# Two layers of a decoder on one core: low parts, constant products and statistics at the layer norms moved

## Chip, core and metric

The kernel runs on one core of one Trainium2 chip. The metric is the device time of one execution in microseconds (us), the median over the runs.

## What is computed

A trunk of two layers makes one inference step for 512 prompt tokens and 8 sample tokens, held as one matrix of 520 columns and 1024 rows. Layer 0 mixes with a gated convolution and a matrix memory, layer 1 with two kinds of sparse attention; after each mixer and each MLP there is a layer norm over a scaled residual:

```python
yp = layer_norm(ALPHA * yp + mp, ln_g[layer, 0], ln_b[layer, 0])
yp = layer_norm(ALPHA * yp + sq_relu_mlp(yp, w_up[layer], w_down[layer]), ln_g[layer, 1], ln_b[layer, 1])

def layer_norm(x, g, b):
    mu = jnp.mean(xf, axis=-1, keepdims=True)
    var = jnp.mean(jnp.square(xf - mu), axis=-1, keepdims=True)
    y = (xf - mu) * lax.rsqrt(var + LN_EPS) * g + b

def sq_relu_mlp(x, w_up, w_down):
    return jnp.square(jax.nn.relu(x @ w_up)) @ w_down
```

The same holds for the sample tokens (`ys`). The MLP is 1024 x 4096 and back.

## The kernel before

Activations lie transposed: `xT` has the 1024 features in 8 blocks `k` of 128 partitions and the 520 tokens in two halves of 260 columns. Half 0 and half 1 go through the chip one behind the other wherever a norm stands between two matrix products.

Every large product is computed in three parts, since each operand is split into a rounded high part and the rest: high weight times high x, high weight times low x, low weight times high x. For an output tile of 128 rows and one half this makes 24 matmuls (8 blocks `k` times 3), each of 260 columns. High parts are written by ScalarE (ACT): `wr` for weights, `xh` for activations. Low parts are a subtraction: `ring_lo` for weights, by VectorE (DVE, `w_lo`, L2081), and `xl` for activations, by DVE (L2179) for the blocks 0, 2, 4, 6, 7 and by GpSimd (POOL, `x_low`, L854) for the blocks 1, 3, 5. Weights come from HBM in chunks of four tiles (2 MB) into three slots, loaded by SyncE's queue (SP) when the tile that used the slot last is done.

There are three such norms with a split result: norm 0 (behind the output projection of layer 0, ahead of its MLP), norm 1 (behind that MLP, ahead of layer 1's input projection) and norm 2 (behind the output projection of layer 1, ahead of its MLP). Ahead of a norm stands a "tail" on TensorE (PE): 8 tiles for half 0, then the same 8 tiles for half 1. Behind it stands a "head": 8 tiles of the MLP for half 0, then the same for half 1, of which the first four run together, block `k` by block `k`.

While the tail's tiles come out, each engine does its part of the norm, in an order that is written out by hand, one queue for each engine, with semaphores between them:

- DVE adds each tile to the residual (`residual`, L2092 and L2093). Between the tiles of half 1 it also works on half 0: `normed` (times 1/deviation, L2160), `x_lows` (L2177, L2179), and the low weights of the head's first four tiles (L2081).
- ACT squares the residual (L1705). Between the tiles of half 1 it scales half 0 (`scaled`, L1750), which gives `xh` and the blocks 1, 3, 5, 7 of `xT`, and copies the head's first weights (L1679).
- POOL adds up sums and squares over the tiles (`sums`, L820 to L825, two additions a tile), subtracts the mean from half 0 (`centre`, L832) and makes its three low parts (`x_low`, L854), one each behind the sums of tiles 4, 5 and 6 of half 1.
- PE multiplies the sums with a constant matrix `meanM` (`norm_sums`, the statistics): those of half 0 behind the first tail tile of half 1, those of half 1 behind head tile 0. They wait for POOL's last addition of the half.

At the start of the head PE also issues products of two constant matrices whose result nobody reads (`keep_busy`, L1027): 5 ahead of head tile 0 and 10 ahead of its block 2 at norms 0 and 2, 14 and 10 at norm 1. In the trace each of them is two instructions.

In the MLP's first part the other engines run `hidden(j)` for the head's tiles of half 0: ACT's relu, the copy of the weights of head tile j + 4 and the square `hh`; POOL's product `hid` (L866); DVE's low weights of tile j + 4 and the subtraction `hl` (L2110). Between them stand the steps of half 1 of the norm: ACT `moments`, `deviation`, `scaled`; DVE `variance`, `inverse`, `normed`, `x_lows`; POOL `centre`, `x_low`. Before the change `moments` and `variance` are the first thing in the queue, ahead of `hidden(0)`.

Head tile `i` from 4 on waits until ACT has read the bank of tile `i - 4`; in half 1 the same holds for DVE.

Of the kernel before, what the change touches and what calls it, by code (L numbers as in the profile page):

```python
# [29 lines left out]
KD = D // P  # L30
# [39 lines left out]
XL_POOL = (1, 3, 5)  # L70
# [7 lines left out]
def build(nc, x_prompt, x_sample, state_conv, state_C, state_n, state_m, cache_kv, cache_idx, cache_win, page_table,  # L78
# [20 lines left out]
    with ExitStack() as ctx:  # L99
# [522 lines left out]
        for branches, pairs in ((("d",), ((3, 0), (2, 1))), (("s", "w"), ((2, 0), (1, 3)))):  # L622
            for pair in pairs:
                for br in branches:
                    heads = [[(p, g) for p in range(NP) for g in range(2)] for _ in pair]
                    for n in last_turns if (pair, br) == ((1, 3), "w") else turns:
                        i = pair[n]
# [129 lines left out]
        def _(pool):  # L757
# [71 lines left out]
            def centre(n_ln, half, ms):  # L829
                pool.wait_ge(sm["mu_ok"], 2 * n_ln + half + 1)  # L830
                for m in ms:
                    pool.tensor_tensor(xT[:, m, cols(half)], xT[:, m, cols(half)], mu[:, cols(half)],  # L832
                                       ALU.subtract).then_inc(sm["cen_p"], 1)

            def norm(n_ln, g0):

                for i, (m, half) in enumerate(norm_order(n_ln)):
                    if m:
                        sums(n_ln, g0, m, half)
                    if (m, half) == (KD - 1, 0):  # L840
                        centre(n_ln, 0, range(KD))
                    if 2 * KD - 4 <= i < 2 * KD - 1:
                        x_low(n_ln, 0, (XL_POOL[i - 2 * KD + 4],))

            def split_y(k, s, v, y=ymix, at=0):

# [3 lines left out]
            def x_low(n_ln, half, ms):  # L850
                c = cols(half)
                for m in ms:
                    pool.wait_ge(sm["x_ready"], xr(n_ln, half) + XT_ACT.index(m) + 1)
                    pool.tensor_tensor(XL[n_ln][:, m, c], xT[:, m, c], XH[n_ln][:, m, c].bitcast(F32), ALU.subtract).then_inc(sm["xl_p"], 1)  # L854
# [13 lines left out]
            def mlp(layer, g):  # L868

                n_ln = 2 * layer  # L870
                for j in range(KD):
                    hidden(layer, g + j, 0, j, 0)
                    if j < 2:
                        centre(n_ln, 1, range(4 * j, 4 * j + 4))
                    if 3 <= j < 6:
                        x_low(n_ln, 1, (XL_POOL[j - 3],))
                for j in range(KD):
                    hidden(layer, g + j, 0, j, 1)
                for c in range(1, NFC):
                    for j in range(KD):  # L880
                        hidden(layer, g + 2 * KD * c + j, c, j)
# [7 lines left out]
            for idx in range(len(E_TILE)):  # L889
                g = G_IN0 + idx  # L890
                if 17 <= idx < 21:
                    i = idx - 17
# [125 lines left out]
        def _(pe):  # L1018
# [8 lines left out]
            def keep_busy(bank, n):  # L1027

                for _ in range(n):
                    mm(ps[bank][:, 0:P], ident[:, :], ones[:, :])  # L1030
# [57 lines left out]
            def head(n_ln, g):  # L1088

                n = HEADS[g]  # L1090
                keep_busy(3, 14 if n_ln == 1 else 5)
                hi_here = x_hi_here(n_ln, 0)

                def first_tile(k):
                    if k == 2:
                        keep_busy(3, 10)
                    hi_here(k)

                for i in range(n):
                    if i >= 4:  # L1100
                        pe.wait_ge(sm["free_a"], g + i - 3)
                    split_pass((g + i,), (0,), XH[n_ln], XL[n_ln], first_tile if i == 0 else None,
                               x_lo_here(n_ln, 0) if i == 0 else None)
                    if i == 0:
                        norm_sums(n_ln, 1)
                first = n // 2
                split_pass(range(g, g + first), (1,), XH[n_ln], XL[n_ln], x_hi_here(n_ln, 1), x_lo_here(n_ln, 1))
                for i in range(first, n):
                    if i >= 4:
                        pe.wait_ge(sm["free_b"], g + i - 3)  # L1110
                    split_pass((g + i,), (1,), XH[n_ln], XL[n_ln])
# [278 lines left out]
            for idx, name in enumerate(O_NAMES):  # L1390
# [6 lines left out]
                if 4 <= idx <= 6:  # L1397

                    n = idx - 4
                    i = 3 - n  # L1400
# [273 lines left out]
        def _(act):  # L1674
# [51 lines left out]

            def mlp(layer, g):
                n_ln = 2 * layer
                moments(n_ln, 1)
                for j in range(KD):  # L1730
                    hidden(layer, g + j, 0, j, 0)
                    if j == 0:
                        deviation(n_ln, 1)
                    if 1 <= j <= 4:
                        scaled(n_ln, 1, (2 * j - 2, 2 * j - 1))
                for j in range(KD):
                    hidden(layer, g + j, 0, j, 1)
                for c in range(NFC):
                    for j in range(KD if c else 0):
                        hidden(layer, g + j, c, j)  # L1740
                    g += KD
                    for j in range(KD if c < NFC - 1 else 0):
                        w_hi_ahead(g + j)
                    g += KD
                if layer == 0:
                    norm(1, g - KD)
# [6 lines left out]
            def moments(n_ln, half):  # L1753

                act.wait_ge(sm["stats_mm"], 2 * n_ln + half + 1)
                copy(mu[:, cols(half)], ps[4 * half][:, 0:H2]).then_inc(sm["mu_ok"], 1)
                act.activation(var[:, cols(half)], ps[4 * half][:, 0:H2], ACT.Square).then_inc(sm["sq_mu"], 1)

            def deviation(n_ln, half):
                act.wait_ge(sm["std_in"], 2 * n_ln + half + 1)  # L1760
                act.activation(rs[:, cols(half)], var[:, cols(half)], ACT.Sqrt).then_inc(sm["stats_ok"], 1)

            def scaled(n_ln, half, ms):

                for m in ms:
                    act.wait_ge(sm["cen_v"], KD * (2 * n_ln + half) + m + 1)
                    affine(XH[n_ln], n_ln, m, half).then_inc(sm["x_hi"], 1)
                    act.wait_ge(sm["x_hi"], KD * (2 * n_ln + half) + m + 1)
                    if m in XT_ACT:
                        affine(xT, n_ln, m, half).then_inc(sm["x_ready"], 1)  # L1770
# [172 lines left out]
            for idx, name in enumerate(O_NAMES):  # L1943
# [8 lines left out]
                if 4 <= idx <= 6:  # L1952
                    n = idx - 4
                    i = 3 - n
# [56 lines left out]
            for t in range(len(units) + 5):  # L2011
                if t < len(units):
                    i, p, g, br, k0, o = units[t]
# [9 lines left out]
                if 0 <= u < len(units):  # L2023
                    i, p, g, br, k0, o = units[u]
# [44 lines left out]
        def _(dve):  # L2069
# [43 lines left out]

            def mlp(layer, g):
                n_ln = 2 * layer
                variance(n_ln, 1)
                for j in range(KD):
                    hidden(layer, g + j, 0, j, 0)
                    if j == 0:
                        inverse(n_ln, 1)  # L2120
                    if j <= 4:
                        normed(n_ln, 1, NORMED[n_ln][j])
                        x_lows(n_ln, 1, LOWS[n_ln][j])
                for j in range(KD):
                    hidden(layer, g + j, 0, j, 1)
                for c in range(NFC):
                    for j in range(KD if c else 0):
                        hidden(layer, g + j, c, j)
                    g += KD
                    scale = ALPHA if c == 0 else None  # L2130
                    if c < NFC - 1:
                        for m in range(KD):
                            for half in range(2):
                                residual(g, m, half, scale)
                            w_lo_ahead(g + m)
                        g += KD
                    elif layer == 0:
                        norm(1, g, scale)
                    else:
                        last_norm(g)  # L2140

            def variance(n_ln, half):

                c = cols(half)
                dve.wait_ge(sm["sq_mu"], 2 * n_ln + half + 1)
                link(dve.tensor_tensor(var[:, c], ps[4 * half + 1][:, 0:H2], var[:, c], ALU.subtract))
                dve.tensor_scalar(var[:, c], var[:, c], 0.0, LN_EPS, ALU.max, ALU.add).then_inc(sm["std_in"], 1)

            def inverse(n_ln, half):
                dve.wait_ge(sm["stats_ok"], 2 * n_ln + half + 1)  # L2150
                dve.reciprocal(rs[:, cols(half)], rs[:, cols(half)]).then_inc(sm["std_ok"], 1)  # L2151

            def normed(n_ln, half, ms):

                c = cols(half)
                dve.wait_ge(sm["std_ok"], 2 * n_ln + half + 1)
                for m in ms:
                    x = xT[:, m, c]
                    dve.wait_ge(sm["cen_p"], KD * (2 * n_ln + half) + m + 1)
                    dve.tensor_tensor(x, x, rs[:, c], ALU.mult).then_inc(sm["cen_v"], 1)  # L2160

            def x_lows(n_ln, half, ms):
                for m in ms:
                    if m in XL_DVE:
                        x_low(n_ln, half, m)
# [239 lines left out]
            for idx, t in enumerate(E_TILE):  # L2405
# [40 lines left out]
                if idx >= 25:  # L2446
                    i = idx - 25
# [440 lines left out]
```

## Time and profile before

| | us |
|---|---|
| median of 3 runs | 1395.46 (1393.62 to 1395.48) |
| the profiled execution | 1396.67 |
| its span, first to last instruction | 1395.1 |

| engine | busy us | share of the span |
|---|---|---|
| PE, matmul | 1349.7 | 97% |
| PE, weight load | 1286.0 | 92% |
| DVE | 722.7 | 52% |
| ACT | 506.0 | 36% |
| POOL | 395.2 | 28% |

The profile comes from one execution. Busy time is the union of an engine's instructions; the end of a matmul is modelled, and matmuls overlap in the pipeline, so starts are the better measure on PE. "Granted clock" is the share of TensorE's full clock (2.4 GHz) that it was given; its mean is 0.988. In a timeline a bracket gives the idle time of the engine ahead of the instruction and the instruction that released it. Lines are those of the kernel before.

### The profile page before, as it was taken

How to read it: one execution, taken by the hardware profiler on the slowest of the kernel's cores; microseconds unless marked ns; L12 is line 12 of the kernel's file. 1: busy time of each engine (PE TensorE's matmuls, PEld its weight loads, DVE VectorE, ACT ScalarE, POOL GpSimd, SP SyncE). 2: the span in 40 equal slices, each digit the busy share in tenths (PEclk: the TensorE clock that was granted, in tenths of full speed). 3: DMA queues.
4: the chain of work that ended last, by engine and by line, in shares of the span. 5: the costliest groups of instructions: out<-in, count | busy, mean ns of one | idle time of the engine just before them, and what ended most of it. 6: DMA issues, size and time to landing. Idle time of an engine off the chain costs nothing. (4 is left out here: it accounts for less than half of the span.)

```text
span 1395.1 us, 27563 instructions
## 1 busy us (share of the span) xinstructions
PE 1349.7 (97%) x11310; PEld 1286.0 (92%) x11310; DVE 722.7 (52%) x1390; ACT 506.0 (36%) x1014; POOL 395.2 (28%) x467
## 2 busy tenths in 40 slices
PE   5999999999999999999999999999999999999996
PEld 5999999999999999999899766668999999999996
DVE  3425966774343343446789655553674343333435
ACT  3322236454031231234442467775453131230311
POOL 3013535652010010137534371025651010110102
PEclk9999999999999999999999899999999999999998
DMA  5351251213313131304331154212303222222201
GB/s 159 100 143 61 91 188 65 71 52 121 122 61 121 62 121 61 122 8 99 99 62 37 33 170 129 62 44 79 122 19 123 102 87 96 93 89 99 84 31 62
DMA packets 87101, 123.87 MB, mean 89 GB/s; under 512 B 24338, under 2 KB 42206, under 8 KB 86944
## 3 DMA queue, kind: packets, MB, share of 16 engines
q1 hardware_dynamic: 82048, 107.00, 24.0%
q0 software_dynamic: 4928, 15.10, 3.6%
q8 instruction: 91, 1.49, 0.4%
q14 instruction: 34, 0.28, 0.1%
HBM read 115.62 MB, written 8.57 MB: 89 GB/s over the span
## 5 line engine op out<-in xcount | busy, mean ns | idle before, releaser
L1063 PE MATMUL ps<-xh,ring_lo 128*128 128x260 f32 (+2 forms) x2496 | 504.6, 284 | 0.0
L1063 PEld LDWEIGHTS ps<-xh,ring_lo 128*128 128x128 f32 (+2 forms) x2496 | 383.6, 187 | 1.5 <-ACT big L1679 0.4
L1063 PE MATMUL ps<-xl,wr 128*128 128x260 f32 x1568 | 351.8, 283 | 6.1 <-DVE xl L2179 3.8
L1063 PE MATMUL ps<-xh,wr 128*128 128x260 f32 x1568 | 353.4, 284 | 1.4 <-DVE ring_lo L2081 1.0
L1063 PEld LDWEIGHTS ps<-xl,wr 128*128 128x128 f32 x1568 | 255.6, 188 | 7.8 <-DVE xl L2179 5.0
L1063 PEld LDWEIGHTS ps<-xh,wr 128*128 128x128 f32 x1568 | 256.3, 188 | 3.5 <-ACT att L1716 1.4
L866 POOL TENSOR_TENSOR att<-att 128x520 f32<-128x520 f32 (+1 forms) x80 | 77.3, 967 | 548.5 <-DVE att L2105 521.5
L2081 DVE TENSOR_TENSOR ring_lo<-ring,wr 128x1024 fp32r<-128x1024 f32 (+1 forms) x144 | 192.0, 1336 | 60.2 <-ACT wr L1679 60.1
L1063 PE MATMUL ps<-hh,wr 128*128 128x260 f32 x1024 | 222.1, 283 | 0.0
L1063 PE MATMUL ps<-hh,ring_lo 128*128 128x260 f32 x1024 | 221.8, 283 | 0.0
L1063 PE MATMUL ps<-hl,wr 128*128 128x260 f32 x1024 | 221.7, 283 | 0.0
L1679 ACT ACTIVATE wr<-ring 128x1024 fp32r<-128x1024 f32 (+1 forms) x162 | 167.9, 1050 | 130.0 <-PE ps L1063 119.7
L1063 PEld LDWEIGHTS ps<-hh,wr 128*128 128x128 f32 x1024 | 164.5, 188 | 0.2 <-issue 0.2
L1063 PEld LDWEIGHTS ps<-hh,ring_lo 128*128 128x128 f32 x1024 | 164.5, 188 | 0.0
L1063 PEld LDWEIGHTS ps<-hl,wr 128*128 128x128 f32 x1024 | 164.0, 188 | 0.0
L1716 ACT ACTIVATE att<-ps 128x260 f32<-128x260 f32 x64 | 24.6, 384 | 304.5 <-PE ps L1063 304.5
L2092 DVE TENSOR_TENSOR xT<-xT,ps 128x260 f32<-128x260 f32 x96 | 37.5, 421 | 162.9 <-PE ps L1063 162.9
L2105 DVE TENSOR_SCALAR att<-ps 128x260 f32<-128x260 f32 x64 | 27.3, 427 | 137.5 <-PE ps L1063 137.5
L1063 PE MATMUL ps<-hl,ring_lo 128*128 128x260 f32 (+1 forms) x464 | 93.5, 283 | 0.0
L1679 ACT ACTIVATE big<-ps 128x260 f32<-128x260 f32 (+6 forms) x104 | 40.3, 401 | 138.9 <-PE ps L1063 121.6
L813 POOL TENSOR_TENSOR ring_lo<-ring,wr 128x1024 fp32r<-128x1024 f32 x18 | 43.3, 2412 | 108.5 <-ACT wr L1679 108.5
L1025 PE MATMUL ps<-big 128*64 128x128 f32 (+3 forms) x504 | 67.0, 353 | 4.7 <-DVE small L2843 3.3
(356 smaller groups left out, 1581.1 us busy)
## 6 DMA issues: line engine op xcount, KB each, us to landing
ring<-in_w_up SPq DMA_DIRECT2D x16, 2048.0 KB, 7.9
ring<-in_w_down SPq DMA_DIRECT2D x16, 2048.0 KB, 7.9
ring<-in_w_in_e SPq DMA_DIRECT2D x9, 1024.0 KB, 6.8
ring<-in_w_in_e SPq DMA_DIRECT2D x2, 2048.0 KB, 8.7
ring<-in_w_out_e SPq DMA_DIRECT2D x2, 2048.0 KB, 9.4
ring<-in_w_in_o SPq DMA_DIRECT2D x16, 256.0 KB, 4.9
ring<-in_cache_kv POOLq DMA_DIRECT2D x32, 128.0 KB, 2.4
ring<-in_w_out_o SPq DMA_DIRECT2D x8, 512.0 KB, 7.9
```

The lines of the kernel that those rows point to most:

```text
L813: pool.tensor_tensor(w_l, w_raw(u), w_h.bitcast(F32), ALU.subtract).then_inc(sm["w_lo_p"], 1)
L866: pool.tensor_tensor(hid[j % 2][:, cc], rel[j % 2][:, cc], rel[j % 2][:, cc], ALU.mult).then_inc(sm["hid_sq"], 1)
L1025: return pe.matmul(out, lhsT, rhs, start=start, stop=stop, skip_group_check=True)
L1063: last = pe.matmul(bank(g, half)[0:width(g), 0:H2], w[:, k, :], x[:, k, cols(half)], start=first, stop=final)
L1679: return act.activation(out, in_, ACT.Copy, scale=scale)
L1716: act.activation(rel[j % 2][:, 0:H2], psA(g)[:, 0:H2], ACT.Relu).then_inc(sm["free_a"], 1)
L2081: dve.tensor_tensor(w_l, w_raw(u), w_h.bitcast(F32), ALU.subtract).then_inc(sm["w_lo"], 1)
L2092: last = (dve.tensor_tensor(x, x, y, ALU.add) if scale is None else dve.scalar_tensor_tensor(x, x, scale, y, ALU.mult, ALU.add))
L2105: dve.tensor_scalar(rel[j % 2][:, H2:T], psB(g)[:, 0:H2], 0.0, None, ALU.max).then_inc(sm["free_b"], 1)
```

## The change

Three things change at norms 0 and 2; norm 1 stays as it is. POOL's three low parts of half 0 stand behind the sums of tiles 3, 4 and 5 of half 1. PE issues no constant products there. The statistics of half 1 stand behind head tile 1, and the steps of half 1 on ACT, DVE and POOL move one hidden tile back in their queues, so that `hidden(0)` stands ahead of `moments` and `variance`, and POOL's `centre` and `x_low` of half 1 stand one hidden tile later. The steps of half 1 move in the two MLPs, which stand behind norms 0 and 2.

```diff
@@ POOL, norm
-                    if 2 * KD - 4 <= i < 2 * KD - 1:
-                        x_low(n_ln, 0, (XL_POOL[i - 2 * KD + 4],))
+                    late = i - 2 * KD + (4 if n_ln == 1 else 5)
+                    if 0 <= late < 3:
+                        x_low(n_ln, 0, (XL_POOL[late],))
@@ POOL, mlp
                     hidden(layer, g + j, 0, j, 0)
-                    if j < 2:
-                        centre(n_ln, 1, range(4 * j, 4 * j + 4))
-                    if 3 <= j < 6:
-                        x_low(n_ln, 1, (XL_POOL[j - 3],))
+                    if 1 <= j < 3:
+                        centre(n_ln, 1, range(4 * j - 4, 4 * j))
+                    if 4 <= j < 7:
+                        x_low(n_ln, 1, (XL_POOL[j - 4],))
@@ PE, head
-                keep_busy(3, 14 if n_ln == 1 else 5)
+                if n_ln == 1:
+                    keep_busy(3, 14)
                 def first_tile(k):
-                    if k == 2:
+                    if k == 2 and n_ln == 1:
                         keep_busy(3, 10)
...
-                    if i == 0:
+                    if i == (0 if n_ln == 1 else 1):
                         norm_sums(n_ln, 1)
@@ ACT, mlp
-                moments(n_ln, 1)
                 for j in range(KD):
                     hidden(layer, g + j, 0, j, 0)
                     if j == 0:
+                        moments(n_ln, 1)
+                    if j == 1:
                         deviation(n_ln, 1)
-                    if 1 <= j <= 4:
-                        scaled(n_ln, 1, (2 * j - 2, 2 * j - 1))
+                    if 2 <= j <= 5:
+                        scaled(n_ln, 1, (2 * j - 4, 2 * j - 3))
@@ DVE, mlp
-                variance(n_ln, 1)
                 for j in range(KD):
                     hidden(layer, g + j, 0, j, 0)
                     if j == 0:
+                        variance(n_ln, 1)
+                    if j == 1:
                         inverse(n_ln, 1)
-                    if j <= 4:
-                        normed(n_ln, 1, NORMED[n_ln][j])
-                        x_lows(n_ln, 1, LOWS[n_ln][j])
+                    if 1 <= j <= 5:
+                        normed(n_ln, 1, NORMED[n_ln][j - 1])
+                        x_lows(n_ln, 1, LOWS[n_ln][j - 1])
```

## Rows read from the trace of the kernel before

**Rows 1.** The page, part 1: busy us, share of the span, instructions of each engine.

```profile
PE 1349.7 (97%) x11310; PEld 1286.0 (92%) x11310; DVE 722.7 (52%) x1390; ACT 506.0 (36%) x1014; POOL 395.2 (28%) x467
```

**Rows 2.** Timeline of PE: start, us, line, out<-in, count [idle before <-releaser].

```profile
276.17 1.28 PE L1025 MATMUL ps<-ones,ident 128*128 128x128 f32 x10
...
278.00 2.39 PE L1025 MATMUL ps<-ones,ident 128*128 128x128 f32 x20
280.15 0.36 PE L1063 MATMUL ps<-xh,wr 128*128 128x260 f32 x1
...
282.84 0.39 PE L1063 MATMUL ps<-xl,wr 128*128 128x260 f32 x1 [1.25 <-POOL xl L854]
...
284.24 1.15 PE L1025 MATMUL ps<-att,meanM 128*128 128x260 f32 x4 [0.17 <-POOL att L825]
285.03 0.47 PE L1063 MATMUL ps<-xh,wr 128*128 128x260 f32 x1
...
1009.29 1.15 PE L1025 MATMUL ps<-att,meanM 128*128 128x260 f32 x4 [0.17 <-POOL att L825]
```

**Rows 3.** Timeline of POOL at norm 0.

```profile
272.07 0.80 POOL L822 TENSOR_TENSOR att<-att,xT 128x260 f32<-128x260 f32 x1 [2.23 <-DVE xT L2093]
...
273.84 0.75 POOL L854 TENSOR_TENSOR xl<-xT,xh 128x260 fp32r<-128x260 f32 x1
...
278.24 0.81 POOL L854 TENSOR_TENSOR xl<-xT,xh 128x260 fp32r<-128x260 f32 x1
280.54 0.74 POOL L822 TENSOR_TENSOR att<-att,xT 128x260 f32<-128x260 f32 x1 [1.49 <-DVE xT L2093]
...
282.05 0.73 POOL L854 TENSOR_TENSOR xl<-xT,xh 128x260 fp32r<-128x260 f32 x1
282.74 0.74 POOL L822 TENSOR_TENSOR att<-att,xT 128x260 f32<-128x260 f32 x1
```

**Rows 4.** Timelines of DVE, PE and POOL in the head behind norm 0.

```profile
297.90 1.22 DVE L2081 TENSOR_TENSOR ring_lo<-ring,wr 128x1024 fp32r<-128x1024 f32 x1
...
303.19 0.36 PE L1063 MATMUL ps<-xh,wr 128*128 128x260 f32 x1 [0.52 <-DVE ring_lo L2081]
...
306.15 0.64 PE L1063 MATMUL ps<-xh,wr 128*128 128x260 f32 x4
...
307.41 0.93 POOL L854 TENSOR_TENSOR xl<-xT,xh 128x260 fp32r<-128x260 f32 x1
```

**Rows 5.** Timeline of DVE: low parts without and with POOL at work.

```profile
270.03 0.43 DVE L2179 TENSOR_TENSOR xl<-xT,xh 128x260 fp32r<-128x260 f32 x1
...
273.95 0.92 DVE L2179 TENSOR_TENSOR xl<-xT,xh 128x260 fp32r<-128x260 f32 x1
```

**Rows 6.** Timeline of ACT at norm 0: last squares, hidden(0).

```profile
280.50 0.75 ACT L1705 ACTIVATE att<-xT 128x260 f32<-128x260 f32 x2 [3.70 <-DVE xT L2093]
...
285.97 0.40 ACT L1716 ACTIVATE att<-ps 128x260 f32<-128x260 f32 x1
286.24 1.07 ACT L1679 ACTIVATE wr<-ring 128x1024 fp32r<-128x1024 f32 x1
```

**Rows 7.** Windows: stretch, us, busy PE, PEld, DVE, ACT, POOL, clock, DMA share, GB/s.

```profile
272.00:274.00 2.00, 2.00 (x19) 2.00 (x18) 1.97 (x4) 1.62 (x4) 1.85 (x3) 1.00 0.04 11
282.00:284.00 2.00, 1.16 (x8) 1.03 (x8) 0.00 (x0) 0.00 (x0) 1.95 (x3) 1.00 0.74 277
664.00:667.00 3.00, 2.95 (x13) 2.86 (x14) 2.22 (x4) 0.00 (x0) 0.00 (x0) 0.50 0.03 5
785.00:790.00 5.00, 5.00 (x23) 3.85 (x23) 1.60 (x5) 1.41 (x3) 2.18 (x4) 0.50 0.08 13
```

**Rows 8.** Timelines of DVE and POOL: low weights of a tile, POOL's instruction behind.

```profile
287.35 1.63 DVE L2081 TENSOR_TENSOR ring_lo<-ring,wr 128x1024 fp32r<-128x1024 f32 x1
...
287.86 1.73 POOL L832 TENSOR_TENSOR xT<-xT,att 128x260 f32<-128x260 f32 x1
```

**Rows 9.** Waits of PE from 304 to 654 us: total, times, longest.

```profile
PE ps L1063 <- DVE att L2105: 0.2, 1, 0.2
```

## The prediction

> **What bounds the kernel now.** I read the page's busy line first: TensorE (PE) is busy 97% of the span [rows 1], so only time in which PE waits, or works for nothing, can be won. Then the timelines of the engines around norm 0. Norm 2 shows the same picture 725 us later, row for row within 0.1 us (its statistics row is the last of [rows 2]); one set of rows stands for two norms.
>
> On PE [rows 2] the tail's last tile of half 1 is followed by 10 constant instructions at 276.17, by products k = 0 and 1 of head tile 0, by 20 constant instructions from 278.00 to 280.15, and by k = 2 to 5. There PE waits 1.25 us, until 282.84, for xl of k = 5; about 1.07 us later tile 0 is through, and at 284.24 the statistics of half 1 start, released by POOL's last addition. POOL [rows 3] shows why k = 5 is late: its three subtractions (273.84, 278.24, 282.05) stand behind the sums of tiles 4, 5 and 6, and those wait for DVE's residuals. PE reaches half 1 of the head at 306.15, 21.91 us after the statistics, with one more wait in between: 0.52 us at 303.19 for the low weights of head tile 7, a DVE product [rows 4].
>
> **The constants.** They cost what they occupy: 20 in 2.15 us, so 10 in 1.07, together 3.2 us a norm [rows 2]. Taken alone this wins nothing certain, since PE may only wait instead. The sum must go by what ends last, and that is POOL's and DVE's chain.
>
> **The low parts.** The subtraction for k = 1 moves behind the sums of tile 3, into the gap of 2.23 us that ends at 272.07; k = 3 takes the slot of 273.84, k = 5 that of 278.24, and the slot at 282.05 falls away [rows 3]. So k = 5 would be ready at 279.05 (278.24 + 0.81) instead of 282.78. The new slot is not free: in that gap DVE has a subtraction of its own, at 270.03, which took 0.43 us with POOL idle, while the one at 273.95, begun 0.11 us after a POOL subtraction, took 0.92 [rows 5]. I charge the difference, 0.5 us, to the DVE chain behind it, which had no gap up to the residuals that release POOL at 280.54 [rows 3]; the bounds are 0 and 0.5. POOL's sums of tiles 6 and 7 come 0.5 us later with them; k = 5 is ready at 279.57.
>
> PE then starts tile 0 at 276.17 and needs xl of k = 5 after five times three products of 0.12 us, at 278.1. It waits 1.5 us until 279.63, ends tile 0 at 280.70 (1.07 us, as before) and tile 1 at 283.61. For the 2.91 us of a tile: tiles 1 to 6 took from 285.03 to 303.19 less the wait there, which is 0.52 us by its row and 0.16 more because a row's end is modelled, 0.28 us after a start where the next can start after 0.12 [rows 2, 4].
>
> **Statistics behind tile 1.** They need POOL's sums of tile 7. Two additions and the wait between them take 1.5 us (280.54 to 282.05 for tile 6), then tile 7's, without the subtraction of 0.69 [rows 3]. With DVE's 0.5 us the statistics would start 0.17 us sooner than before, at 284.07.
>
> Here the reordering adds a cost. ACT's and DVE's work for hidden tile 0 now stands ahead of the statistics, and nothing holds it. ACT's squares (two from 280.50) move to 281.0, its relu follows at 281.7, and 0.27 us behind it the copy of the weights of head tile 4, 1.07 long, which ends at 283.0 [rows 6]. Their load is through by 272, when the DMA share is down to 0.04 [rows 7]; SP's queue is not moved. DVE then asks for its 1.21 us product for these low weights at 283.06. POOL's first addition for tile 7 runs from 282.57 to 283.3. So DVE asks while POOL is at work, between two additions. The trace has this meeting: DVE's same product began at 287.35 under a POOL subtraction and ended at 288.98, and POOL's next one took 1.73 us, where one without DVE takes 0.74 [rows 3, 8]. POOL's second addition would start 0.7 us behind the first, at 283.27, and last until 285.0; the statistics start at 285.05, 0.81 us later than before. The Trainium skill, in "SBUF — State Buffer", section "Who interferes with whom", has it that GpSimd and a VectorE instruction with two SBUF inputs share a read port as an exclusive lock, and that the later one stands still until the first is through. The rows agree (1.73 against 0.74 us); without such a lock the statistics would start at 284.07, as in the first rival below. Of the two values I take 285.05, because DVE's request comes some 0.1 us before POOL's first addition frees the port. That margin is thin.
>
> POOL's hidden product for tile 0 fits behind its last addition, and DVE's subtraction for it ends before ACT has read the statistics, so the chain of variance, root, reciprocal, centring and scaling keeps its distance from the statistics; each hidden tile in it has an index one higher. So the low weights of tile 7 stand where those of tile 6 stood, ready at 299.12, 14.88 us after the statistics [rows 4], while PE comes to tile 7 after 0.79 + 5 × 2.91 = 15.3 us. The wait at 303.19 goes, with 0.4 us to spare. Half 1 of the head starts 0.79 + 6 × 2.91 = 18.25 us after the statistics, not 21.91. Late next is POOL's low part k = 5 of half 1. It ended at 308.34, 24.1 us after the statistics [rows 4], and keeps that place; PE, which takes 12 × 0.12 = 1.43 us for a k of four tiles, wants it after 18.25 + 5 × 1.43 + 0.48 = 25.9 us. It is hidden with 1.8 us to spare; beyond that it would cost its full lateness.
>
> **The sum.** A norm gains 21.91 − 18.25 = 3.66 us less the lateness of the statistics, 0.81: 2.85 us. Two norms: 5.7 us. From there to norm 1 PE waits once more, 0.2 us [rows 9], so the gain goes through to the end; norm 1 keeps its constants and places. Against the profiled run of 1396.67 us (span 1395.1, 1.6 us around it) this gives 1391.0; that run lies 1.2 us above the median of 1395.46, so I forecast 1389.8. By the bounds (DVE 0 or 0.5 us late, the meeting or not) a norm gains between 2.85 and 4.35 us.
>
> **Rivals.** (1) POOL's last addition gets the port before DVE's weight product, because ACT's copy ends 0.2 us later than I have it. Statistics at 284.07: 3.83 us a norm, 7.7 us, 1387.8; without the 0.5 us on DVE as well, 4.35 a norm, 8.7 us, 1386.8. For it: the thin margin. Against it: ACT's and POOL's times hang on the same residual, so they don't drift apart.
>
> (2) The change does not do what it says: POOL meets two DVE instructions, not one, in its last sums. A second meeting costs about another 1.0 us (1.73 − 0.74), the gain is 1.85 a norm, 3.7 us: 1391.8. Against it: after its last residual DVE has nothing but the weight product to do there.
>
> (3) The clock. The constants keep PE at work in the gap. At norm 1, from 664 to 667, the granted clock was 0.50, the 1.2 GHz level, in spite of constants [rows 7]. If such a fall follows at norms 0 and 2, 3 us at half speed lose 1.5 us each: 5.7 − 3.0 = 2.7 us, 1392.8. Against it: norm 0 before waits 1.25 and 0.17 us at full clock (1.16 busy of the 2 us from 282), and the forecast has two gaps of 1.5 us with 4 us of dense products between. The Trainium skill's page "TensorE: Matmul & The Clock Gate", section "Why this matters for your kernels", warns of idle gaps between bursts, after which the clock goes back to half; the row at 664 agrees.
>
> (4) Slower than before: the clock stays at the low level for longer, as from 785 to 790, where it was 0.50 over all 5 us with PE busy throughout [rows 7]. Two such rows after each norm, 10 us, lose 5 us each, 10.0 − 5.7 = 4.3 us: 1399.8. It decides from 5.7 us at half speed in each norm on. Against it: there PE ran 23 products in 5 us, here they are dense.
>
> **How the numbers follow.** Forecast 0.50 (its own range 1389.0 to 1391.0), rival 1 0.28, rival 2 0.08, rival 3 0.08, rival 4 0.06. The range 1386.5 to 1392.5 takes in the forecast, rivals 1 and 2 and the bounds: 0.86. About 0.2% (2.8 us) is what a measurement of this kernel can tell from no change: faster 0.50 + 0.28 + 0.08 = 0.86; same, rival 3, 0.08; slower, rival 4, 0.06.
>
> **What would show it.** In the changed kernel's timeline: no constants at norms 0 and 2; PE's wait at k = 5 about 1.5 us, now beginning near 278.1; statistics behind tile 1 near 285.05 with a wait of about 1.4 us on POOL's addition (near 284.1 in rival 1); one POOL addition of 1.7 us beside DVE's weight product; no wait at tile 7; half 1 of the head near 303.3 (302.3 in rival 1) and no wait for a low part in it; granted clock 1.00 from 276 to 310. A second wait on POOL in half 1, or a stretch at 0.50, would make the prediction wrong.

## The result, and the profile after

| | changed | before, measured beside it |
|---|---|---|
| median (range) of 5 runs, us | 1386.89 (1384.80 to 1387.99) | 1393.85 (1393.52 to 1395.48) |
| ratio, 95% interval | 0.9945 [0.9931, 0.9959] | |
| profiled execution, its span | 1387.08, 1385.5 | 1396.67, 1395.1 |
| mean granted clock | 0.991 | 0.988 |

Three of the five runs of before are those of the forecast; the two new ones took 1393.52 and 1393.85 us. The change makes the kernel faster by about 0.55% by the ratio; the medians differ by 7.0 us, 0.50%. The median lies 2.9 us under the forecast of 1389.8, 2.1 us below the forecast's own range (1389.0 to 1391.0) and 0.4 us inside the wide one; two of the five runs lie below the wide range. At the norms nearly every row landed where the prediction had it; the other 2.9 us lie elsewhere.

The busy line of the changed kernel, against [rows 1]; TensorE (PE) has lost its 60 constant instructions:

```profile
PE 1338.3 (97%) x11250; PEld 1275.7 (92%) x11250; DVE 722.7 (52%) x1390; ACT 505.6 (36%) x1014; POOL 397.0 (29%) x467
```

PE's waits from 254 to 320 us in the changed kernel (total, times, longest), and its timeline there, against [rows 2, 4]. The tail ends 1.06 us earlier in this execution, at 275.11 instead of 276.17, because its start was 1.1 us quicker; times below have to be shifted by that.

```profile
PE ps L1026 <- POOL att L825: 1.3, 1, 1.3
PE ps L1064 <- POOL xl L855: 1.3, 1, 1.3
PE ps L1064 <- DVE att L2108: 0.2, 1, 0.2
```

```profile
278.51 0.39 PE L1064 MATMUL ps<-xl,wr 128*128 128x260 f32 x1 [1.32 <-POOL xl L855]
...
283.95 1.14 PE L1026 MATMUL ps<-att,meanM 128*128 128x260 f32 x4 [1.33 <-POOL att L825]
...
302.21 0.63 PE L1064 MATMUL ps<-xh,wr 128*128 128x260 f32 x4
```

Two waits are left at the norm: 1.32 us for xl of k = 5 and 1.33 us for POOL's last addition (counted from starts, as the prediction does, 1.5 us each; forecast 1.5 and 1.4). None stands at head tile 7, and half 1 waits for no low part; its one wait, 0.2 us on DVE, is that of [rows 9]. From the end of the tail, k = 5 comes after 3.40 us (forecast 279.63 − 276.17 = 3.46), the statistics after 8.84 (8.88) and half 1 of the head after 27.10 (27.1). From the statistics to half 1 it is 18.26 us, as forecast 18.25, where [rows 2, 4] have 21.91.

POOL and VectorE (DVE) at norm 0 in the changed kernel, against [rows 3, 8]:

```profile
268.84 0.75 POOL L855 TENSOR_TENSOR xl<-xT,xh 128x260 fp32r<-128x260 f32 x1
...
277.65 0.80 POOL L855 TENSOR_TENSOR xl<-xT,xh 128x260 fp32r<-128x260 f32 x1
279.95 0.75 POOL L822 TENSOR_TENSOR att<-att,xT 128x260 f32<-128x260 f32 x1 [1.50 <-DVE xT L2096]
...
281.48 0.75 POOL L822 TENSOR_TENSOR att<-att,xT 128x260 f32<-128x260 f32 x1
282.19 1.71 POOL L825 TENSOR_TENSOR att<-att 128x260 f32<-128x260 f32 x1
```

```profile
268.95 0.92 DVE L2183 TENSOR_TENSOR xl<-xT,xh 128x260 fp32r<-128x260 f32 x1
...
281.92 1.39 DVE L2084 TENSOR_TENSOR ring_lo<-ring,wr 128x1024 fp32r<-128x1024 f32 x1 [1.71 <-ACT wr L1681]
```

POOL's first subtraction sits in the former gap, where DVE's own, at 268.95, now takes 0.92 us instead of the 0.43 of [rows 5]; no subtraction stands between the sums of tiles 6 and 7. The sums of tile 6 begin at 279.95, where 280.54 − 1.06 = 279.48 would be no delay: the DVE chain is 0.47 us late, forecast 0.5. DVE's weight product asks at 281.92 (forecast 283.06 − 1.06 = 282.0), while POOL's first addition for tile 7 is at work, and POOL's second takes 1.71 us (forecast 1.73). The statistics stand 8.84 us behind the tail's end, before 284.24 − 276.17 = 8.07: 0.77 us later, forecast 0.81.

The clock at norm 0 in the changed kernel (stretch, us, PE busy, clock, DMA share, GB/s) stays at the full level through both waits, unlike rival 3:

```profile
275.00:280.00 5.00, 3.68 (x31) 1.00 0.74 238
280.00:285.00 5.00, 3.67 (x27) 1.00 0.49 181
285.00:300.00 15.00, 15.00 (x127) 1.00 0.01 2
```

From the end of the tail to half 1 of the head, norm 0 takes 27.10 us after 29.98, norm 2 takes 26.95 after 29.76: 2.88 and 2.81 us, 5.7 in all, which is the forecast. But the spans differ by 9.6 us. The rest of that: 1.1 at the start of the kernel, 1.6 in the attention stage near 804 us, 1.3 near 947 us. The code there is the same. Before, the clock fell in both of the later places; in the changed kernel's profile it did not:

```profile
800.00:810.00 10.00, 7.77 (x62) 0.83 0.00 2
...
944.00:952.00 8.00, 6.38 (x54) 0.79 0.07 14
```

(before, same columns) and, after,

```profile
800.00:810.00 10.00, 9.74 (x83) 1.00 0.04 13
...
944.00:952.00 8.00, 7.42 (x80) 1.00 0.10 18
```

### The profile page after: what moved, and what is told of

It is laid out like the page before. It is cut to its first block, busy times and chain, and to the rows that moved or that the text cites. A ratio compares the mean times of both kernels' runs of the same rounds, so it can differ in the third digit from the quotient of the medians.

```text
span 1385.5 us, 27443 instructions
## 1 busy us (share of the span) xinstructions
PE 1338.3 (97%) x11250; PEld 1275.7 (92%) x11250; DVE 722.7 (52%) x1390; ACT 505.6 (36%) x1014; POOL 397.0 (29%) x467
## 4 chain that ended last, share of the span: by engine, by line
PE 83%; DVE 12%; issue 2%; ACT 1%; DMA 1%; POOL 0%; SPq 0%; DVEq 0%; ACTq 0%; POOLq 0%
PE ps L1064 69%; PE ps L1026 9%; PE ps L1022 4%; DVE big L2568 2%; DVE small L2567 2%; DVE xT L2164 1%; DVE ring_lo L2084 1%; DMA big<-in_x_prompt 1%; DVE xT L2181 1%; DVE xl L2183 0%; DVE att L2643 0%; DVE big L2554 0%; POOL att L825 0%; ACT att L2021 0%; DVE big L2553 0%
## 5 line engine op out<-in xcount | busy, mean ns | idle before, releaser
L2095 DVE TENSOR_TENSOR xT<-xT,ps 128x260 f32<-128x260 f32 x96 | 37.5, 422 | 162.9 <-PE ps L1064 162.9
L1064 PEld LDWEIGHTS ps<-hl,ring_lo 128*128 128x128 f32 (+1 forms) x464 | 70.3, 185 | 0.6 <-DVE hl L2283 0.2
```

The costliest lines, as they stand in the source:

```text
L1064: last = pe.matmul(bank(g, half)[0:width(g), 0:H2], w[:, k, :], x[:, k, cols(half)], start=first, stop=final)
L2095: last = (dve.tensor_tensor(x, x, y, ALU.add) if scale is None else dve.scalar_tensor_tensor(x, x, scale, y, ALU.mult, ALU.add))
```

## Experiments

All edits are to the changed kernel unless the kernel before is named. Stretches are from the traces: "norms" from the end of the tail to the first product of half 1 of the head, at norm 0 and norm 2; "norm 1" between the same two products of PE, near 650 and 700 us; "attention" likewise, near 775 and 815 us. The ratio is to the kernel before, measured beside the run on the same chip. The chip changes from one group to the next, so medians are compared within a group only: the median of before was 1393.85 beside the changed kernel (profiled), 1393.03 beside again, constants_back, low_weights_held and stats_tile2, 1392.72 beside constants_gone_only, 1392.33 beside low_parts_back, stats_back, delay_4 and delay_8, and 1392.22 beside the others.

| run | median us | ratio, 95% interval | norms us | norm 1 | attention |
|---|---|---|---|---|---|
| before (profiled) | | | 29.98, 29.76 | 50.04 | 39.99 |
| before_1, _2, _3 | one each: 1392.15, 1396.28, 1393.37 | | 29.98 to 30.00, 29.76 to 29.80 | 50.11, 49.97, 50.10 | 38.42, 40.06, 38.40 |
| changed (profiled) | 1386.89 | 0.9945 [0.9931, 0.9959] | 27.10, 26.95 | 50.08 | 38.39 |
| again | 1384.30 | 0.9941 [0.9928, 0.9954] | 27.13, 26.92 | 48.58 | 37.48 |
| again_2 | 1386.36 | 0.9962 [0.9949, 0.9974] | 27.10, 26.94 | 49.91 | 40.04 |
| constants_gone_only | 1395.04 | 1.0011 [0.9999, 1.0022] | 31.52, 31.07 | 48.61 | 38.43 |
| constants_back | 1385.45 | 0.9943 [0.9930, 0.9956] | 27.25, 27.28 | 49.98 | 40.07 |
| low_parts_back | 1393.10 | 1.0010 [0.9998, 1.0022] | 30.11, 30.07 | 49.99 | 37.47 |
| stats_back | 1393.02 | 1.0002 [0.9991, 1.0012] | 31.35, 30.50 | 48.61 | 37.46 |
| low_weights_held | 1385.97 | 0.9947 [0.9934, 0.9961] | 26.13, 25.96 | 50.00 | 37.48 |
| stats_tile2 | 1381.28 | 0.9920 [0.9906, 0.9935] | 25.50, 25.32 | 48.58 | 35.91 |
| stats_tile2_b | 1381.92 | 0.9930 [0.9914, 0.9945] | 25.49, 25.32 | 48.57 | 34.33 |
| delay_4 | 1386.87 | 0.9952 [0.9935, 0.9969] | 27.11, 26.95 | 48.60 | 38.42 |
| delay_8 | 1385.94 | 0.9957 [0.9943, 0.9971] | 27.13, 26.92 | 48.58 | 40.06 |
| before_delay_8 | 1394.55 | 1.0018 [1.0008, 1.0029] | 29.95, 29.79 | 48.57 | 38.37 |
| before_delay_8b | 1394.01 | 1.0017 [1.0008, 1.0026] | 29.95, 29.80 | 48.57 | 37.37 |

### The three parts one by one

**Constants gone, nothing else.** The kernel before with

```diff
-                keep_busy(3, 14 if n_ln == 1 else 5)
+                if n_ln == 1:
+                    keep_busy(3, 14)
...
-                    if k == 2:
+                    if k == 2 and n_ln == 1:
                         keep_busy(3, 10)
```

> The kernel before without its constant products at norms 0 and 2, nothing else. Theory: PE waits for k = 5 as long as the constants took and 1.25 us more, the statistics start where they did, stretch 29.9 us, gain 0 from the norms. Rival (constants cost what they occupy): 26.8 us a norm, 6.4 us less in all. Rival (clock): PE is idle for 4.5 us at one go, the clock falls to 0.50 behind it and the norm is 1 to 2 us longer than before.

PE's timeline and three windows of its clock (columns as above):

```profile
277.35 0.39 PE L1064 MATMUL ps<-xl,wr 128*128 128x260 f32 x1 [1.55 <-POOL xl L855]
...
281.07 0.58 PE L1064 MATMUL ps<-xl,wr 128*128 128x260 f32 x1 [2.74 <-POOL xl L855]
```

```profile
274.00:280.00 6.00, 2.79 (x22) 1.00 0.63 237
280.00:287.00 7.00, 5.93 (x23) 0.52 0.26 96
287.00:292.00 5.00, 5.00 (x43) 0.99 0.01 2
```

PE waits 1.55 us for k = 3 and 2.74 us for k = 5, two gaps and not the one of 4.5 us that was expected. The clock falls to its lower level, 0.50, during the second and stays there for 6.8 us. The norms get 1.5 and 1.3 us longer, although 3.2 us of useless products are gone from each. That is the mechanism of rival 3, in a part of the change instead of the whole. The total hardly shows it: its interval takes in no change (norm 1 was 1.4 us shorter in this execution).

**Constants put back into the changed kernel** (the same lines the other way round).

> The changed kernel with the constant products of norms 0 and 2 back. Theory: POOL's and DVE's chain ends last, so the constants fill waits: no wait for k = 5, tile 1 ends 9.3 us after the tail, statistics 0.45 us later than in the changed kernel, stretch 27.5 us, 0.9 us more in all. Rival (the constants are what cost): 3.2 us a norm, stretch 30.3 us, 6.4 us more.

```profile
274.41 1.28 PE L1026 MATMUL ps<-ones,ident 128*128 128x128 f32 x10
...
276.24 2.39 PE L1026 MATMUL ps<-ones,ident 128*128 128x128 f32 x20
```

Neither the wait for k = 5 nor the one for the statistics is left. The norms are 0.15 and 0.33 us longer than in the changed kernel, the time is the same within the spread of the runs. So taking the constants out is worth some 0.5 us in all.

The constants do more here than fill gaps. ACT, POOL and DVE at norm 0 of this run:

```profile
280.83 0.39 ACT L1717 ACTIVATE att<-ps 128x260 f32<-128x260 f32 x1 [0.84 <-PE ps L1064]
```

```profile
281.50 0.75 POOL L825 TENSOR_TENSOR att<-att 128x260 f32<-128x260 f32 x1
282.33 1.57 POOL L867 TENSOR_TENSOR att<-att 128x260 f32<-128x260 f32 x1
```

```profile
282.19 1.22 DVE L2083 TENSOR_TENSOR ring_lo<-ring,wr 128x1024 fp32r<-128x1024 f32 x1 [2.67 <-ACT wr L1680]
```

With them PE ends tile 0 later, ACT's relu waits 0.84 us for it, and DVE's weight product comes only when POOL's last addition is nearly through: the addition takes 0.75 us (at norm 2 as well), and at norm 0 it is POOL's next product that takes long, 1.57 us. So the meeting at POOL's last addition comes with taking the constants out, and the 0.5 us is what is left when its price is paid. Without constants and without the meeting (low_weights_held, below) the norms take 26.13 and 25.96 us, 1.1 and 1.3 us less than here.

**Low parts back in their old places**, without constants and with the statistics behind tile 1:

```diff
-                    late = i - 2 * KD + (4 if n_ln == 1 else 5)
+                    late = i - 2 * KD + 4
```

> The changed kernel with POOL's low parts of half 0 back behind the sums of tiles 4, 5 and 6. Theory with the clock: as in the run without constants only, PE waits 1.5 us for k = 3 and 2.7 us for k = 5 with nothing between, the granted clock falls to 0.50 behind it, and the stretch from the tail to half 1, 28.9 us at full clock (tile 1 ends 10.6 us after the tail), becomes 31 to 32 us: 2 to 4 us slower than the kernel before at the norms. Theory without it: 28.9 us, 2.2 us less than before.

PE's waits from 254 to 310 us and its clock:

```profile
PE ps L1064 <- POOL xl L855: 4.3, 2, 2.7
```

```profile
281.00:285.00 4.00, 3.69 (x19) 0.57 0.24 87
```

The same waits as with the constants gone alone, and a fall of the clock of 3.4 us. The norms are back at 30.11 and 30.07 us; the sum from waits at full clock was 28.9. The 31 to 32 us expected with the clock did not come; the fall lasted half as long as with the constants gone alone.

**Statistics back behind tile 0**, with all steps of half 1 in their old places:

```diff
-                    if i == (0 if n_ln == 1 else 1):
+                    if i == (0 if n_ln == 1 else 0):
                         norm_sums(n_ln, 1)
...
```

> The changed kernel with the statistics of half 1 back behind tile 0, and the steps of half 1 back in their old places. Theory of the chain: POOL's last addition ends 7.9 us after the tail, PE waits 1.3 us for k = 5 and 3.3 us for the statistics, stretch 29.8 us at full clock; with a fall of the clock behind the 3.3 us, 31 to 32 us. Rival (the low parts and the constants carry the gain, the place of the statistics does not): 27 to 28 us.

```profile
PE ps L1026 <- POOL att L825: 3.2, 1, 3.2
PE ps L1064 <- POOL xl L855: 1.3, 1, 1.3
```

```profile
281.00:288.00 7.00, 5.12 (x19) 0.52 0.20 73
```

Here the two waits, 1.3 and 3.2 us, follow each other with little between them, and the clock falls again, for 6.8 us at norm 0 and 3.4 us at norm 2. So with the constants gone, either of the other two parts left out gives the whole gain back. The reverse does not hold: with the constants kept, the two other parts carry all but some 0.5 us of the gain. What each of these two is worth alone, with the constants kept, was not run.

### The meeting at the port

One wait on DVE, ahead of the weight product of hidden tile 0, holds it until POOL's last addition is done:

```diff
+                if (c, j, half) == (0, 0, 0):
+                    dve.wait_ge(sm["sum_r"], sum_event(2 * layer, KD - 1, 1))
```

> DVE's low weights of head tile 4 wait until POOL's last sums of half 1 are done. Theory of the shared port: POOL's last addition is back at 0.74 us (1.71 in the changed kernel), the statistics come 0.95 us sooner, PE's wait there shrinks from 1.3 to about 0.35 us, the stretch from the tail to half 1 is 26.2 us instead of 27.1, 1.9 us less in all than the changed kernel; up to 0.4 us a norm may come back as a wait for the low weights of tile 7. Rival (the sums are late for another reason, ACT's squares or DVE's residual): the addition stays, the time too.

POOL, then DVE, then PE's waits from 254 to 320 us, with DVE held:

```profile
281.56 0.75 POOL L822 TENSOR_TENSOR att<-att,xT 128x260 f32<-128x260 f32 x1
282.27 0.73 POOL L825 TENSOR_TENSOR att<-att 128x260 f32<-128x260 f32 x1
283.07 1.66 POOL L867 TENSOR_TENSOR att<-att 128x260 f32<-128x260 f32 x1
```

```profile
283.03 1.22 DVE L2084 TENSOR_TENSOR ring_lo<-ring,wr 128x1024 fp32r<-128x1024 f32 x1 [2.75 <-POOL att L825]
```

```profile
PE ps L1064 <- POOL xl L855: 1.3, 1, 1.3
PE ps L1026 <- POOL att L825: 0.4, 1, 0.4
PE ps L1064 <- DVE att L2108: 0.2, 1, 0.2
```

The addition takes 0.73 us instead of 1.71, PE waits 0.4 instead of 1.33, and each norm is about 0.97 us shorter (26.13, 25.96). The long instruction has moved on to POOL's next one, the product at 283.07, which nobody waits for on the path. So the meeting and its price are shown. The total does not show the 1.9 us: 1385.97 against 1384.30 for the changed kernel beside it, with norm 1 1.4 us longer in the profile.

### A better version: statistics behind tile 2

The addition is 1.3 us late for a place behind tile 1; a tile later, 2.91 us, no wait should be left. `norm_sums` stands behind tile 2, and the steps of half 1 on ACT, DVE and POOL go one more tile back:

```diff
-                    if i == (0 if n_ln == 1 else 1):
+                    if i == (0 if n_ln == 1 else 2):
                         norm_sums(n_ln, 1)
...
-                    if 1 <= j < 3:
-                        centre(n_ln, 1, range(4 * j - 4, 4 * j))
-                    if 4 <= j < 7:
-                        x_low(n_ln, 1, (XL_POOL[j - 4],))
+                    if 2 <= j < 4:
+                        centre(n_ln, 1, range(4 * j - 8, 4 * j - 4))
+                    if 5 <= j < 8:
+                        x_low(n_ln, 1, (XL_POOL[j - 5],))
...
```

> Statistics of half 1 one more tile later, and the steps of half 1 one more hidden tile back, at norms 0 and 2. Theory: PE no longer waits for POOL's last addition (1.3 us a norm), half 1 of the head starts 25.7 us after the tail instead of 27.1; but the slack of POOL's low part k = 5 of half 1 (1.8 us by my sum) is used up, so a wait of 0 to 1.2 us appears there. Between 0.4 and 2.8 us less than the changed kernel. Rival: the chain of half 1 was the bound already, no gain.

PE's waits from 254 to 320 us, and POOL's low part k = 5 of half 1:

```profile
PE ps L1064 <- POOL xl L855: 1.3, 1, 1.3
PE ps L1064 <- DVE att L2108: 0.2, 1, 0.2
```

```profile
304.71 0.93 POOL L855 TENSOR_TENSOR xl<-xT,xh 128x260 fp32r<-128x260 f32 x1
```

The wait for the addition is gone, half 1 begins 25.5 us after the tail (1.6 us less), and its k = 5, which ends at 305.64, is there before PE wants it at 299.75 + 5 × 1.43 + 0.48 = 307.4. The slack that was expected to be used up is still 1.8 us, so no wait came in place of the old one, and the gain is above the 0.4 to 2.8 us expected: 3.2 us at the two norms, 3.0 us in the medians against the changed kernel beside it. A repeat against again_2 gave 4.4:

> Statistics behind tile 2 once more, beside the changed kernel on the same chip: norms 0 and 2 at 25.5 and 25.3 us, 3.2 us less than the changed kernel, give or take 2 us for the clock in norm 1 and the attention stage.

It beats both kernels, with 0.9920 and 0.9930 of the time of before.

### What lies outside the norms

The norms give 5.7 us. The changed kernel, run again:

> The changed kernel once more. Theory: each of norms 0 and 2 is 2.85 us shorter (from the end of the tail on PE to half 1 of the head 27.1 us, where it was 30.0), 5.7 us in all; what was measured beyond that is clock level and start, not the norms, and will differ from run to run: falls of the granted clock in the attention stage near 780 to 810 and 947 us come and go, each worth about 1.7 us. Rival: the change itself is worth 7 to 8 us, and every profile shows the missing falls near 804 and 947 us.

The gain was 0.59% (8.2 us), in the first measurement 0.55% (7.7 us), both by the ratio. The rival fails on its second half: the profile of again has a fall near 938 us (granted clock 0.83 from 936 to 946), the stage that stood at 947 before, and that of again_2 one near 800 us (0.79 from 798 to 806). Is the excess of 2 to 2.5 us chance, or a shift of the stages behind the norms? Three single executions of the kernel before:

> The kernel before once more, for a second profile of it. Measured medians differ by 7 to 8.7 us, the two norms by 5.7. Theory A: the rest is in the kernel before, whose waits at norms 0 and 2 let the granted clock fall in some executions: stretches from the tail to half 1 of 31 us or more, with a window at 0.50 in them. Theory B: the rest is chance outside the norms: both stretches are again 29.8 to 30.0 us at full clock, and what differs is the start, norm 1 and the attention stage, where the profile of before had four falls of the clock.

(For before_2 and before_3 the same two theories were put on record.) The norms of all four profiles of before agree within 0.04 us, without a fall: theory B. Attention took 38.4 or 40.1 us, the start of the kernel 26.5 to 28.2 (to the same product of PE), and the spans 1390.5 to 1394.7: this is chance. All other stretches of PE (the first MLP, from norm 1 to attention, behind norm 2) agree within 0.1 us over these and the three profiles of the changed kernel, apart from the one around 947 us (185.1 us from attention to norm 2 without its fall, 186.3 with it). So the excess can lie only in the start, norm 1, attention and that fall. Only norm 1 was constant, with its fall of the clock in all four profiles of before, in two of the three of the changed kernel. To test whether this fall hangs on when norm 1 is reached, PE got n constants ahead of the third up-projection of layer 0 (0.86 us for n = 4, 1.72 us for n = 8), in the changed kernel and in the one before:

```diff
+                        if (layer, c) == (0, 2):
+                            keep_busy(7, 8)
```

> The changed kernel with 4 constant products (0.86 us) in the middle of the first MLP, far from any norm. If the falls of the clock in norm 1 and in the attention stage fall by chance, run by run, the time is 0.9 us more than that of the changed kernel. If they hang on when those stages are reached, the time moves by something else, between 4 us less and 4 us more, with norm 1 at 48.6 or at 50.1 us and the attention stage between 36 and 40 us; norms 0 and 2 stay at 27.1 and 26.9 us either way.

> As the one before, with 8 constant products (1.72 us) in the middle of the first MLP: 1.7 us more than the changed kernel if the falls come by chance; something else, up to 4 us away, if they hang on when norm 1 and the attention stage are reached. Norms 0 and 2 stay at 27.1 and 26.9 us.

> The kernel before with 8 constant products (1.72 us) in the middle of the first MLP. If the fall of the clock in norm 1 hangs on when norm 1 is reached (it was there in all four profiles of the kernel before, in one of the four of the changed kernel with and without a delay), it is gone here: norm 1 takes 48.6 us instead of 50.0, and the time is about 0.2 us more than before. If the fall comes by chance or belongs to the kernel before as such, norm 1 is at 50.0 us in most profiles and the time is 1.7 us more.

> The same kernel again, for a second profile: norm 1 at 48.6 us if the fall hangs on when norm 1 is reached; at 50.0 us if it belongs to the kernel before as such.

Norm 1 in windows of PE (columns as above), first before, then the kernel before with the delay:

```profile
655.00:670.00 15.00, 11.62 (x81) 0.89 0.80 138
```

```profile
655.00:670.00 15.00, 11.63 (x93) 1.00 0.81 142
```

In all four delayed kernels norm 1 took 48.6 us, as it did without a delay in constants_gone_only, stats_back and stats_tile2, where a norm ahead is longer or shorter. Yet the kernel before was not faster for it: it lost 0.17 to 0.18%, some 2.4 us, where 0.2 was expected for a fall saved. The intervals, 1.1 to 4.0 and 1.1 to 3.6 us, take in the 1.72 of the delay. What the delay costs the changed kernel in all can't be said: no changed kernel ran beside delay_4 and delay_8, and their ratios, 0.9952 and 0.9957, lie among its own three. In one of the two traces (an execution of 1396.02 us) a fall stands further on instead, with a granted clock of 0.83 in the window from 838 to 848 us; the other, without it, is the fastest of its ten executions (1390.81 us, median 1394.01). So the fall at norm 1 moves with small things ahead of it, but the total shows no gain from a saved fall. The third measurement of the changed kernel was

> The changed kernel a third time: norms 0 and 2 at 27.1 and 26.9 us. The measured gain over the kernel before stays at 7 to 8 us if stages outside the norms give the rest, with norm 1 at 48.6 us in part of the executions; it comes back to 5.7 us if the earlier medians were chance.

0.9962 [0.9949, 0.9974], a gain of 5.3 us (3.6 to 7.1), on the 5.7 of the norms. The three gains are 7.7, 8.2 and 5.3 us by the ratio, 7.1 in the mean (by the medians 7.0, 8.7 and 5.9). Whether 1 to 2 us of them belong to the change by way of norm 1 or are chance is not settled.

## Why the prediction was right and wrong

**Right: the path at the norms.** Low parts: k = 5 after 3.40 us, forecast 3.46, with the DVE chain 0.47 us late for 0.5. Statistics: 0.77 us late for 0.81, and for the reason given, as the held DVE shows (0.97 us a norm back when the meeting is taken away, where rival 1 priced 3.83 − 2.85 = 0.98). Tile 7: no wait. Half 1: 18.26 for 18.25 us. k = 5 of half 1 hidden. The norms gain 2.88 and 2.81 us for 2.85 each. Rivals 1 and 2 did not come: there was one meeting, not none and not two. The time alone would have misled here: 1386.89 us is what rival 1 asked for (1386.8 to 1387.8), and only the trace, with its addition of 1.71 us, rules it out.

Two readings on this path were off without weight. Norm 2 does not repeat norm 0 "row for row within 0.1 us": its wait for k = 5 was 1.0 us, not 1.25, and its stretch 0.2 us shorter. And the "some 0.1 us" by which DVE's request comes ahead of the end of POOL's first addition is 0.2 by the prediction's own times (283.06 and 283.27); it measured 0.3 (281.92 and 281.48 + 0.75).

**Wrong: the last step, "so the gain goes through to the end", with the base that it was taken from.** The prediction put everything outside the norms at nothing: it took those stages to last as long as in the one profiled execution, and 1395.46, from three runs, for the level of before. The rows that it cites for the step, [rows 9], are PE's waits up to 654 us; they show neither the clock nor what lies behind. The miss of 2.9 us splits so: with two more runs the median of before was 1393.85, 1.6 us lower (and 1392.2 to 1393.0 later, on other chips, so the base was high); and the medians differ by 7.0 us, 1.3 more than the norms give. Nothing in the forecast stood for either. That the median still fell inside the wide range is luck: the range was made for rivals at the norms, and none of them came. What the 1.3 us are, a part of the change or chance, stays open. Four profiles of the same code show attention from 38.4 to 40.1 us and the start from 26.5 to 28.2. The profile of before had drawn long ones: 39.99 and 28.20. A fall of the clock stood in [rows 7] at 664 and at 785, and I used those rows only as a price for a new fall, not as a sign that the old ones could come and go. A range that went 1 to 2 us further down could have followed from them.

**Too mild: the step on the constants.** "Taken alone this wins nothing certain, since PE may only wait instead" has a worse end that the prediction put at another place: alone it loses 1.5 and 1.3 us a norm by rival 3's mechanism, the fall of the clock. In the whole change the fall did not come, and that fits the reason the prediction gave against rival 3: two gaps of 1.3 us with 4 us of dense products between them. In the five profiles with these two gaps (the changed kernel's three, delay_4 and delay_8) none of the ten norm stretches has a fall. With 2.7 or 3.2 us in one gap, and another gap shortly ahead, all six have one. No run separates the length of the second gap from the nearness of the two. The constants had been paying for themselves, and it took both other parts to make them superfluous. Taking them out then gains 0.5 us, because it also brings on the meeting at the port: the cost that the prediction laid to the reordering alone does not come while the constants stand.

Rival 4, the slower one, did not come: the changed kernel has no fall at the norms, and the longest there in a kernel with a part of the change lasted 6.8 us, with a ratio of 1.0011 [0.9999, 1.0022].

The Trainium skill, "SBUF — State Buffer", section "Who interferes with whom", has GpSimd and a VectorE instruction with two SBUF inputs exclude each other at the shared port. The runs agree: 1.71 us beside the DVE product, 0.73 without it, and the 1.66 us on the next POOL instruction once DVE was held.

## What to carry to other kernels

Price a reordering by the last wait on the path and by what two engines will do at the same port then; both came out within 0.1 us from rows of before. Taking work off one engine can bring another's request forward into such a meeting, so price the parts of a change together. For the total, take the level of before from many runs, and the length of stages that the change does not touch from more than one trace: here they alone move it by 1 to 2 us, as much as a part of the change. Before taking filler work off TensorE, ask what gaps it leaves: here two of 1.1 to 1.4 us with 4 us of products between them kept the clock, and 1.2 to 1.6 us close ahead of 2.7 to 3.2 did not.

## What the runs showed of the hardware that was not expected

- The granted clock went from 1.00 (2.4 GHz) to 0.50 (1.2 GHz) in the second of two gaps close together, or within 1 us behind it (1.2 to 1.6 and then 2.7 to 3.2 us, six norm stretches), for 3.4 or 6.8 us; behind 1.32 and 1.33 us with 4 us of products between it stayed at 1.00. At norm 1 it fell in one run and not in another with no PE wait over 1.4 us in either.
- By the times, a DVE instruction that asked while POOL was at work came ahead of POOL's next one, though that was queued right behind: in the changed kernel POOL's first addition ended on time (0.75 us), DVE's product, begun 0.3 us ahead of that end, took 1.39 us for 1.22, and POOL's second addition 1.71.
- One program's stages differ from execution to execution: attention took 38.4 to 40.1 us in the four profiles of before and 37.5 to 40.0 in the three of the changed kernel, with the same code there (over all kernels here 34.3 to 40.1); the start of the kernel took 25.4 to 28.2.
